# Routed rows of the last tile added on the tensor engine, and a gate broadcast moved behind the last early weights

## The reference, cut to what matters

```
x  = x + g1 * (concat([attn, rec]) @ w_out)
h2 = modulate(rms_norm(x, norm2), sh2, sc2)
group  = argmax(softmax(h2 @ wg + bg))              # 4 groups
expert = top_k((h2 @ we + be)[group], 2)            # 2 of the group's 8 experts
act = silu(h2 @ w_gate[e]) * (h2 @ w_up[e]) * weight[e]
y   = x + g2 * sum over the two experts of act @ w_down[e]
```

## Time and profile before

| | |
|---|---|
| median of three runs | 610.94 us |
| the profiled execution: time, span | 611.43 us, 609.6 us |
| granted TensorE clock, mean | 0.997 of full speed |
| busy: PE, DVE, ACT, POOL | 95%, 57%, 30%, 18% |
| chain that ended last: PE, DMA | 76%, 15% |
| mean DMA rate over the span | 302 GB/s of HBM traffic |

### The profile page before, as it was taken

One profiled execution on the slowest core, in us unless ns is written; L12 is line 12 of the kernel. 1 busy time (PEld: TensorE's weight loads), 2 busy tenths in 40 slices (PEclk: granted clock), 3 DMA queues, 4 the chain that ended last, 5 costly groups with the idle time before them and its releaser, 6 DMA issues.

```text
span 609.6 us, 9282 instructions
## 1 busy us (share of the span) xinstructions
PE 581.9 (95%) x3274; PEld 325.0 (53%) x3275; DVE 346.5 (57%) x787; ACT 180.5 (30%) x377; POOL 109.0 (18%) x130
## 2 busy tenths in 40 slices
PE   5989999999998899999999999999999999997996
PEld 2544455455565667644555555555555555555452
DVE  2745898764464987754776787432433243322256
ACT  4203787711144877741101111111111111111110
POOL 4000011121242100000000001322232222221242
PEclk9999999999999999999999999999999999998999
DMA  8999833540018917809311999999999999999997
GB/s 323 379 368 360 325 132 145 206 153 1 1 37 236 341 44 227 357 24 395 151 53 47 373 380 394 405 419 417 420 417 392 414 417 422 420 418 417 418 386 306
DMA packets 48498, 175.89 MB, mean 289 GB/s; under 512 B 11633, under 2 KB 17789, under 8 KB 35408
## 3 DMA queue, kind: packets, MB, share of 16 engines
q1 hardware_dynamic: 36816, 155.06, 64.8%
q0 software_dynamic: 6688, 15.42, 7.2%
q10 hardware_dynamic: 4960, 4.96, 2.4%
HBM read 163.11 MB, written 21.14 MB: 302 GB/s over the span
## 4 chain that ended last, share of the span: by engine, by line
PE 76%; DMA 15%; SPq 3%; DVE 3%; issue 2%; ACTq 1%; ACT 0%; DVEq 0%; POOLq 0%
PE ps L1912 17%; PE ps L1690 11%; PE ps L1935 9%; PE ps L1615 9%; PE ps L1603 7%; PE ps L1730 4%; PE ps L1757 4%; DMA gate_w<-lru_wx 3%; DMA y_rows<-w,slot_row_now 3%; DMA w<-h_rows,slot_token 3%; PE ps L1739 3%; PE ps L1872 3%; DMA w_mod_ring<-w_mod 2%; PE ps L1578 2%; SPq L380 2%; PE ps L1524 2%
## 5 line engine op out<-in xcount | busy, mean ns | idle before, releaser
L1912 PE MATMUL ps<-expert_w,hT_mixT 128*64 128x256 f32 x1120 | 135.6, 391 | 4.3 <-issue 4.2
L1912 PEld LDWEIGHTS ps<-expert_w,hT_mixT 128*64 128x64 f32 x1120 | 85.2, 136 | 57.6 <-issue 14.1
L1603 PE MATMUL ps<-hT_mixT,w 128*128 128x128 f32 (+1 forms) x256 | 72.6, 437 | 1.2 <-DVE hT_mixT L999 1.2
L1690 PE MATMUL ps<-w,hT_mixT 128*128 128x512 f32 x160 | 71.9, 597 | 0.0
L1935 PE MATMUL ps<-expert_w,hT_mixT 128*64 128x512 f32 x276 | 66.0, 599 | 0.4 <-ACT hT_mixT L803 0.4
L798 ACT ACTIVATE hT_mixT<-ps 128x128 f32<-128x128 f32 x36 | 10.0, 278 | 177.8 <-PE ps L1912 177.8
L1603 PEld LDWEIGHTS ps<-hT_mixT,w 128*128 128x128 f32 x256 | 38.9, 191 | 35.8 <-issue 32.6
L1435 DVE SCALAR_TENSOR_TENSOR w<-ps,hT_mixT,w 128x1024 f32<-128x1024 f32 x17 | 21.8, 1284 | 57.8 <-PE ps L1935 50.3
L1615 PE MATMUL ps<-w_qkv,hT_mixT 128*128 128x512 f32 (+1 forms) x160 | 53.1, 488 | 0.0
L1388 DVE SCALAR_TENSOR_TENSOR hT_mixT<-hT_mixT,ps 128x128 f32<-128x128 f32 x36 | 10.4, 288 | 66.6 <-ACT hT_mixT L798 66.6
L1690 PEld LDWEIGHTS ps<-w,hT_mixT 128*128 128x128 f32 x160 | 29.1, 191 | 29.9 <-issue 29.7
(11 more groups left out here) (311 smaller groups left out, 757.4 us busy)
## 6 DMA issues: line engine op xcount, KB each, us to landing
expert_w<-exp_w_down SPq DMA_DIRECT2D x30, 1024.0 KB, 17.7
expert_w<-exp_w_gate SPq DMA_DIRECT2D x27, 1024.0 KB
expert_w<-exp_w_up SPq DMA_DIRECT2D x27, 1024.0 KB
w_mod_ring<-w_mod SPq DMA_DIRECT2D x14, 1024.0 KB, 6.5
y_rows<-zero_rows POOLq DMA_DIRECT2D x10, 512.0 KB, 6.1
expert_w<-y_rows SPq DMA_DIRECT2D x10, 512.0 KB, 8.9
recurrence<-w_mod SPq DMA_DIRECT2D x8, 512.0 KB, 9.6
w<-w_in SPq DMA_DIRECT2D x4, 1024.0 KB, 16.8
```

Of the source, the lines that this page charges most:

```text
L1603: ins = pe.matmul(ps[:, bank, 0:n], w1v[:, c, m * P:(m + 1) * P], HM[:, c, lo:lo + n], start=(c == 0), stop=(c == DC - 1))
L1690: ins = pe.matmul(ps[:, 2 * (t % 2) + half, :], HM[:, c, t * P:(t + 1) * P], w1v[:, c, half * 512:(half + 1) * 512], start=(c == 0), stop= ...
L1912: ins = pe.matmul(ps[r, 2 + k, 0:2 * P].rearrange("p (k f) -> p k f", k=2), xT[:, c, r], gate_up(i)[:, :, c, k:FF:FC], start=(c == 0), sto ...
```

## The change

Two things change. First, PE waits for step 0's gather ahead of `rank` of the last tile, transposes `xg` into PSUM banks 0 and 1 without ending the sum there, and later adds the last tile's rows right into the transposed sum by eight products of 128 columns with `h2_last_row` as weights and `first_slot` moving. DVE's addition, the semaphores `late_mm` and `late_ok` and the later transposes go; one of the four `keep_clock` products ahead of `rank` goes; `slot_tokens` stands one column chunk later in step 0. Second, the two copies of `g2` move from behind the gate weights of expert 4 to behind the gate weights of expert 5 (then L477).

```diff
@@ SyncE
             sp.dma_start(ring[:, HOME[4], 0:EW], wg_v[4]).then_inc(wgu_in[2], 16)
-            for i, v in enumerate((1, 0)):
-                sp.dma_start(g2[:, i, :], a["mod_rows"][v, 5 * D:6 * D].partition_broadcast(P)).then_inc(S["g2_in"], 16)
             sp.wait_ge(S["x1T_v"], NT)
             w_down(sp, 5, 5)
...
             sp.dma_start(ring[:, HOME[5], 0:EW], wg_v[5]).then_inc(wgu_in[2], 16)
+            for i, v in enumerate((1, 0)):
+                sp.dma_start(g2[:, i, :], a["mod_rows"][v, 5 * D:6 * D].partition_broadcast(P)).then_inc(S["g2_in"], 16)
             sp.wait_ge(last_rows, 16)
-            sp.wait_ge(S["late_mm"], 2)
+            sp.wait_ge(S["xt_mm"], 2)
@@ VectorE
-            dve.wait_ge(S["xg_in"], 16)
-            for half in range(2):
-                part = xg_row[:, :, 4 * half:4 * half + 4]
-                dve.wait_ge(S["late_mm"], half + 1)
-                dve.tensor_tensor(part, part, ps[:, 5 + half, :].rearrange("p (n c) -> p n c", c=4), ALU.add).then_inc(S["late_ok"], 1)
             ranked(last_tile)
@@ TensorE
-            keep_clock(4)
+            keep_clock(3)
+            pe.wait_ge(S["gated"], 2 * NT)
+            pe.wait_ge(S["xg_in"], 16)
+            for c in range(DC):
+                pe.matmul(ps[:, c // 4, (c % 4) * P:(c % 4 + 1) * P], xg[:, c:D:DC], ident[:, :],
+                          start=(c % 4 == 0), stop=False, is_transpose=True)
             rank(NT - 1)
             keep_clock(1)
             pe.wait_ge(S["h2"], NT)
             pe.wait_ge(S["slot"], TOP * LT + 3)
-            for half in range(2):
-                pe.matmul(ps[:, 5 + half, :].rearrange("p (n c) -> p n c", c=4), first_slot, h2_last_row[:, :, 4 * half:4 * half + 4],
-                          start=True, stop=True).then_inc(S["late_mm"], 1)
+            for c in range(DC):
+                ins = pe.matmul(ps[:, c // 4, (c % 4) * P:(c % 4 + 1) * P], h2_last_row[:, :, c], first_slot,
+                                start=False, stop=(c % 4 == 3))
+                if c % 4 == 3:
+                    ins.then_inc(S["xt_mm"], 1)
...
-                            if routing and half == 0 and k == FC - 1 and c == 1:
+                            if routing and half == 0 and k == FC - 1 and c == 2:
                                 pe.wait_ge(S["slot"], TOP * NT + 4)
...
-            for half in range(2):
-                pe.wait_ge(S["late_ok"], half + 1)
-                turn_half(half)
             with pe.Fori(0, hi) as n:
```

More of the change, by code:

```diff
@@ L253, in build @@
             "out_done v p act xg_in xt_mm gu_mm dn_mm xT_v xT_a th_ok act_ok aT_mm aT_ok y_v idxc_ok pidc_ok y_out "
-            "y_zero gu_half base stepw late_mm late_ok now gsel chosen tail_mm fin sg_ok turn cache_out st_col st_t st_ev").split()}
+            "y_zero gu_half base stepw now gsel chosen tail_mm fin sg_ok turn cache_out st_col st_t st_ev").split()}
         rows_in = [sem(f"rows_in{i}") for i in range(NT)]
```

## The result

The changed kernel takes 614.28 us (median of 15 executions, 612.18 to 618.03), the kernel before, in the same rounds, 611.80 (15 executions, 610.49 to 614.30). The ratio is 1.0042, 95% interval [1.0023, 1.0061]: slower by 0.4%. The forecast was 611.6, its range 609.9 to 613.4. The profiled execution of the changed kernel took 617.41 us with a span of 615.6, so it is one of its longer ones.

The account below looks back on a forecast made before the run. The weights' stream bounds the kernel through step 15's wait, with PE setting it only near 470 us. The later of +0.45 (PE) and +0.7 us (stream) gave 612.1 for the profiled execution, 611.6 for the median; range 609.9 to 613.4.

Parts of the forecast that it names:

- What bounds the kernel: Whole kernel: step 15 waits for pair 13's weights; the end moves by the later of stream shift less slack and PE shift.
- the hole at 470 us: Weights' stream, 470 to 474 us: the one place it runs empty, 468 KB or 1.1 us of slack.
- At this one place PE's progress sets the stream: Pair 9's weights, issued at 470.62 behind step 8's products: elsewhere the stream is set by its own bytes.
- part one: Products onto transposes, around the last tile's rank and step 0: PE's shift +0.45 us, bounds -1.2 and +1.75.
- The nearest row has eight such in 1.95 us: New products on PE: half take 1.0 us, 1.7 from their start to the first gate product, in place of 3.37.
- step 1's gather would be issued 1.2 us earlier: Step 0: slot_tokens at 362.95 in place of 364.17, and steps 1 to 8 move along, if the gather is in time.
- what is free: Step 0's gather ahead of rank: landing up to 355.7 us costs nothing; each us later is a us on rank.
- 359.6 + 1.65: First gate product of step 0: 359.6 with the gather in time, plus 1.65 us for rank starting late at 358.3.
- I take 357.3: Step 0's gather: landing at 357.3 us, 7.2 from its issue, between bounds of 355.7 or earlier and 358.6.
- The starved rival: PE ahead of rank: gather lands at 358.6, PE idles 3.5 us and its clock falls; 613.6 us, chance 0.2.
- Part two: g2 broadcast behind the last weights: stream shifts +1.8 us, bounds +0.3 to +1.8; less 1.1 slack, +0.7.
- dead stretch of 1.6 us at 357 us: DMA engines at 357.3 us: they stand for 1.6 us until the next copy, issued at 357.29, brings its first bytes.

Follow-up runs that it names:

- wait_contig: The changed kernel with each new product's stationary operand 128 numbers side by side instead of every eighth; ratio 1.0014 to the kernel before.
- quiet_gather: The changed kernel with expert 5's down weights moved behind the last gate weights, so nothing is queued right behind the gather; ratio 1.0051 to the kernel before.
- clock_contig: The changed kernel with side-by-side stationary operands and 7 clock-keeping products ahead of the wait in place of 3; ratio 1.0031 to the kernel before.
- after_clock: The changed kernel with 7 clock-keeping products ahead of the wait for the gathered rows in place of 3; ratio 1.0078 to the kernel before.
- only_g2: The kernel before with only the second half of the change, the second gate's rows loaded behind the last weights; ratio 0.9994 to the kernel before.
- before_b: The control: the kernel before with bounds asserted on the loaded step numbers, as in all experiments; ratio 0.9998 to the kernel before.
- only_wait: The kernel before with only the first half of the change, PE's new order, the second gate's rows staying early; ratio 1.0076 to the kernel before.
- change_perm: The changed kernel with VectorE writing the normalised rows with columns turned, so they lie side by side for the products; ratio 1.0097 to the kernel before.
- late_contig: The changed kernel with side-by-side stationary operands and the gather issued later, behind POOL's last power; ratio 1.0082 to the kernel before.

## Why the prediction was wrong

**What bounds the kernel** held in the main. The end moved by PE's shift through step 8 and the refill behind it; the hole at 470 us moved and grew with PE (the profile after), and it was gone where PE was early (from 470 to 482 us wait_contig has 406 to 428 GB/s). "At this one place PE's progress sets the stream" was too narrow: the first refill, at 365.69 before, moved with step 0 as well. And the 15 us for a pair took the rate of all queues; SP's own 29.40 MB in 80 us are 367 GB/s, so 17 us, which leaves the argument as it was.

**The step that failed first** is in part one: "eight products of 128 columns. The nearest row has eight such in 1.95 us". That row has the same shape and type but a stationary operand that lies side by side. Here it is every eighth number, the load takes 335 ns instead of 191, and the 16 records take 4.05 us at full clock. So at full clock the new products cost PE 2.1 us more than I took, whenever the gather lands; instead of "step 1's gather would be issued 1.2 us earlier", step 0 begins 0.6 us late even with the gather nearly in time (quiet_gather). With that one term right, the working of this part is near: a landing of 356.69 in wait_contig, 1.0 us beyond what is free, put step 0 0.49 us ahead of the control, where my working has -1.7 + 1.0, that is -0.7, for the first gate product. The view that shows this was at hand, the weight loads beside the products; I read only the products. The kernel's own rows had the hint as well: in the weight loads before, transposes of every eighth number (L1872) take 195 ns, those of side-by-side rows (L1777) 141.

```profile
L1872 PEld LDWEIGHTS ps<-ident,w 128*128 128x128 f32 x8 | 1.0, 195 | 1.1 <-DVE w L1356 1.1
```

```profile
L1777 PEld LDWEIGHTS ps<-ident,x_tok 128*128 128x128 f32 x32 | 3.7, 141 | 3.4 <-issue 2.1 <-DVE x_tok L1220 1.3
```

And PE, in order, has to issue all eight products ahead of the first gate product, not "a half", as I had it; that is worth 0.25 us.

In the profiled execution my working has the first gate product at 359.6 + 1.65 = 361.25; it came at 366.28. Of these 5.0 us, 2.2 are the rank (360.48 in place of 358.3: the landing 1.3 us later, the transposes slow at the clock of 0.50), 0.7 the clock-keeping product behind it at that clock, and 2.1 the way from the products to the first gate product (3.80 in place of 1.7): there the stride is 0.7 to 0.9, the rest the clock and the half.

The Trainium skill (SBUF — State Buffer, Door 1: The DMA port swizzle) says that SBUF is read in lines of 16 bytes and that an access pattern pays for each step onto a new line, so that f32 can be strided by 4 numbers for free. A stride of 8 numbers goes to a new line each time. The runs agree: 335 against 191 ns for the load, 1059 against 691 for VectorE's writes at a stride of 128 numbers. No run here reads at a stride between 1 and 8, so the 16 bytes themselves are not shown. The rule stood against this change and I had not weighed it.

**The gather's landing.** "I take 357.3": the profiled execution had 358.61. The later runs have 6.5 to 9.6 us from issue to landing with the down weights behind it, so 7.2 was inside, but a single number was the wrong form for it; PE's wait came out at 1.4 to 4.3 us. The reason given, sharing with the down weights, is borne out (5.57 us without them).

**The starved rival**, 0.2 at 613.6, is what the profiled execution shows: a wait of 3.30 us and a clock of 0.50. Its time came near, but it lacked the stride: 0.7 to 0.9 us of PE in such an execution, 2.0 where the clock stays up. What the clock's fall costs by itself stays open: clock_contig (1.0031), in which it did not fall, was not below wait_contig on the same chip (1.0014), in whose profile it did not fall either, and after_clock (1.0078) was not below the changed kernel.

**Part two**, +0.7 us as the later of the two shifts, did not decide the end, and only_g2 does not tell it from zero: 0.9994 [0.9973, 1.0016], that is -1.7 to +1.0 us. The stream did lose what I took: in the 12 us from 3.0 us behind the start of the last logits the queues move 314 GB/s in only_g2 and 371 in before_b, 0.68 MB less, or 1.6 us at 419. But the hole near 470 us, 371 and 219 GB/s from 470 to 474 in before_b, is gone in only_g2 (403 and 414): it took up its 0.5 MB, 1.2 us, as I had it. The broadcast is slow, 219 GB/s (from 360 to 362 us, not the 364 to 368 I had), but no dead stretch of 1.6 us at 357 us appeared (408 and 357 GB/s from 357 to 359 in the profile after). The rows even serve to fill the queue: only_wait, which puts them early again, has 68 GB/s from 366 to 368 us and lost no less than the whole change.

**Range and chances.** The measured time lies 0.9 us above the range. Nearly as much, 0.86, is the kernel before itself, whose median was 611.80 in these rounds and 610.94 in the three runs I started from; but against 611.80 the change costs 2.5 us where I had 0.7. The forecast gave slower 0.32; the misjudged price alone makes PE some 2 us later at full clock, and so PE, not the stream, is what decides.

## What to carry to other kernels

Price a product by a row that has the same layout of its stationary operand, not only its shape and type, and read the weight loads beside the products: where their sum equals the products' busy time, they are the bound. Here the addition in PSUM that replaced one on VectorE turned the operands round, and so the layout that had served the moving side became the stationary side's. And before a wait for a DMA is set ahead of other work on an in-order engine, look at how its landing varies: here it differed by 3 us between executions (of kernels that are alike up to there, on three chips), and everything queued behind it varied with it.

## What the runs showed of the hardware that was not expected

- A float32 weight load of 128x128 takes 191 ns from side-by-side numbers and 335 ns at a stride of 8; a transpose's load 141 and 188 to 205 ns.
- VectorE takes 690 to 692 ns for a float32 multiplication or addition of 128x512 with plain rows and 1039 to 1063 with one operand at a stride of 128 numbers. For 128x1024 with a scalar it takes 1285 ns, and 2080 with one operand (the shift) at a stride of 8.
- A strided load takes 337 ns at a clock of 0.50 and 335 at 1.00, a side-by-side one 334 (change_perm, late_contig) and 191: at the lower clock the stride cost nothing, and where it bounds, the lower clock is hidden.
- The gather's time from issue to landing, the same instruction in the same place, was 6.46 to 9.36 us in seven executions with the weights of one expert queued behind it, and 5.57 without.
